# A transformer pair in one program: the convolution's norm moves one block earlier among a delta rule's blocks, and the first two slabs of the second output projection swap halves

## The reference, cut to what matters

```python
def conformer_conv(a, gate, dw_w, dw_b, ln_g, ln_b):
    y = a * jax.nn.sigmoid(gate)
    y = causal_depthwise_conv(y, dw_w) + dw_b
    y = layer_norm(y, ln_g, ln_b)
    return jax.nn.silu(y)
...
    def step(state, inp):
        u_n, w_n, qk_n, qd_n, kd_n, cd_n = inp
        u = u_n - jnp.einsum("bhck,bhkv->bhcv", w_n, state)
        o = jnp.einsum("bhck,bhkv->bhcv", qd_n, state) + jnp.einsum("bhij,bhjv->bhiv", qk_n, u)
        state = cd_n[..., None, None] * state + jnp.einsum("bhck,bhcv->bhkv", kd_n, u)
        return state, o
...
    o = rms_norm(o, norm_g) * jax.nn.silu(g)
...
        mix = jnp.concatenate([y_a, y_b, y_c], axis=-1)
        x = x + jnp.einsum("bte,ed->btd", mix, w_out[l])
```

## Time and profile before

| what | us |
|---|---|
| median of 3 runs | 3643.97 |
| lowest, highest | 3641.48, 3645.7 |
| the profiled execution, its time | 3644.55 |
| the profiled execution, its span | 3642.7 |
| PE matmul busy | 3535.9 (97%) |
| DVE busy | 1470.6 (40%) |
| POOL busy | 1136.8 (31%) |
| ACT busy | 963.0 (26%) |

### The profile page before, as it was taken

How to read it: one execution, slowest core, us unless ns; L and a number is a source line. 1 busy time by engine, 2 the same in 40 slices (tenths; PEclk the granted TensorE clock), 3 DMA queues, 4 the chain that set the end, 5 groups by cost and what they waited for, 6 DMA issues and landing times.

```text
span 3642.7 us, 52855 instructions
## 1 busy us (share of the span) xinstructions
PE 3535.9 (97%) x20076; PEld 2935.7 (81%) x20076; DVE 1470.6 (40%) x2553; ACT 963.0 (26%) x1684; POOL 1136.8 (31%) x1499
## 2 busy tenths in 40 slices
PE   8999889999999999999999999999999999999998
PEld 6777767888888878899999878797777788888886
DVE  7865455211112163312121473837876521111214
ACT  5243533211111142111111333115663311111112
POOL 4432044322222253222222442310025532222223
PEclk9999999999999999999999999999999999999999
DMA  3111122111111121111111232111024221111113
GB/s 123 41 43 57 34 87 76 59 51 45 53 42 51 40 82 51 48 46 41 52 41 52 58 134 77 41 30 39 30 91 150 87 63 48 51 42 52 46 44 100
DMA packets 79620, 218.51 MB, mean 60 GB/s; under 512 B 18912, under 2 KB 19040, under 8 KB 78816
## 3 DMA queue, kind: packets, MB, share of 16 engines
q1 hardware_dynamic: 61792, 173.35, 15.8%
q10 hardware_dynamic: 17664, 42.88, 3.2%
HBM read 195.67 MB, written 19.46 MB: 59 GB/s over the span
## 4 chain that ended last, share of the span: by engine, by line
issue 61%; POOL 24%; PE 8%; DVE 5%; ACT 1%; POOLq 1%; DMA 0%; ACTq 0%; SPq 0%; DVEq 0%
POOL w_lo L568 24%; PE acc L726 2%; DVE cv_acc L1725 2%; PE acc L727 2%; PE acc L728 2%; PE acc L1267 0%; PE acc L1262 0%; POOLq L572 0%; DVE cvo L1807 0%; DVE ssq L676 0%; DMA x<-in_x_dram 0%; PE acc L1356 0%; PE acc L1277 0%; PE acc L1400 0%; DVE tmp L688 0%
## 5 line engine op out<-in xcount | busy, mean ns | idle before, releaser
L568 POOL TENSOR_TENSOR w_lo<-w_raw,w_hi 128x256 fp32r<-128x256 f32 (+3 forms) x1480 | 1116.1, 786 | 2389.3 <-ACT w_hi L538 2388.9
L726 PE MATMUL acc<-h_hi,w_hi 128*128 128x512 f32 (+1 forms) x3520 | 1304.8, 371 | 25.2 <-POOL w_lo L568 17.6
L727 PE MATMUL acc<-h_lo,w_hi 128*128 128x512 f32 (+1 forms) x3520 | 1303.4, 370 | 0.0
L728 PE MATMUL acc<-h_hi,w_lo 128*128 128x512 f32 (+1 forms) x3520 | 1298.0, 369 | 0.0
L726 PEld LDWEIGHTS acc<-h_hi,w_hi 128*128 128x128 f32 x3520 | 665.2, 189 | 152.8 <-issue 22.1
L727 PEld LDWEIGHTS acc<-h_lo,w_hi 128*128 128x128 f32 x3520 | 664.7, 189 | 118.3 <-issue 1.9
L728 PEld LDWEIGHTS acc<-h_hi,w_lo 128*128 128x128 f32 x3520 | 665.6, 189 | 115.4
L538 ACT CAST w_hi<-w_raw 128x1024 fp32r<-128x1024 f32 (+3 forms) x370 | 346.3, 936 | 1225.0 <-PE acc L728 1205.3
L998 DVE TENSOR_TENSOR ff_hi<-tmp,acc 128x512 f32 (+3 forms) x154 | 94.5, 614 | 1101.6 <-PE acc L728 1066.1
L726 PE MATMUL acc<-ff_hi,w_hi 128*128 128x512 f32 (+1 forms) x1232 | 449.5, 365 | 5.5 <-POOL w_lo L568 2.9
L728 PE MATMUL acc<-ff_hi,w_lo 128*128 128x512 f32 (+1 forms) x1232 | 447.0, 363 | 0.0
(11 more groups left out here) (377 smaller groups left out, 3017.7 us busy)
## 6 DMA issues: line engine op xcount, KB each, us to landing
w_raw<-in_ffn_w_dram SPq DMA_DIRECT2D x94, 512.0 KB, 3.5
w_raw<-in_w_in_dram SPq DMA_DIRECT2D x60, 512.0 KB, 3.6
w_raw<-in_w_out_dram SPq DMA_DIRECT2D x32, 512.0 KB, 3.5
w_raw<-in_ffn_w_dram SPq DMA_DIRECT2D x48, 320.0 KB, 2.9
w_raw<-in_w_gate_dram SPq DMA_DIRECT2D x24, 512.0 KB, 3.5
w_raw<-in_w_up_dram SPq DMA_DIRECT2D x24, 512.0 KB, 3.5
w_raw<-in_ffn_w_dram SPq DMA_DIRECT2D x32, 384.0 KB, 3.1
gates_kept<-gstage ACTq DMA_DIRECT2D x32, 256.0 KB, 2.0
```

The costliest lines, as they stand in the source:

```text
L568: pool.tensor_tensor(w_lo[:, j, a:a + step], w_raw[:, j, a:a + step], w_hi[:, j, a:a + step].bitcast(F32), ALU.subtract).then_inc(split_do ...
L726: pe.matmul(bank, wh, rh, start=(k == 0), stop=False)
L727: pe.matmul(bank, wh, rl, start=False, stop=False)
L728: ins = pe.matmul(bank, wl, rh, start=False, stop=(k == seg.kt - 1))
```

## The change

Four places in the first block, and one in the second.

- `SHARED` and `EXTRA`: m0 is computed before the levels that precede block 0, m1 at the end of block 0 (before: block 1), v0 at the end of block 1 (3), v1 ahead of s0 at the end of block 2 (4). Block 3 keeps only its spread, block 4 its spread and s1.
- DVE: `centred(0)` ahead of block 0 (before: in block 1), `centred(1)` in block 0 (2), `normed(0)` in block 2 (4), `normed(1)` in block 4 (5).
- ACT: both squares of `cv_acc` in block 1, behind the squares of o (before: one each in blocks 2 and 3); the roots v0 in block 1 and v1 in block 2 ahead of s0's; Silu and the high parts in block 5 (6).
- `pe_slab` takes a range of tiles `ks`, and `pe_last`, where `late` is given, runs tiles 0 to 3 of slab 0, tiles 0 to 3 of slab 1, then tiles 4 to 7 of slab 0 and of slab 1.

Nothing is added or left out in PE's, DVE's and POOL's instructions; ACT loads one table less.

```diff
--- before.py
+++ after.py
@@ -702,9 +702,10 @@
             split(0)
             dve.wait_ge(sem("consts_full"), 16)
 
-        def pe_slab(pe, seg, i, j, rhs, only=None, late=None, at=0):
+        def pe_slab(pe, seg, i, j, rhs, only=None, late=None, at=0, ks=None):
 
             n = len(seg.chunks)
+            ks = ks or range(seg.kt)
             fine = only is None
             if not fine:
                 pe.wait_ge(split_done, i * (2 * LOW_PIECES) + LOW_PIECES * (seg.n0 + j + 1))
@@ -716,7 +717,7 @@
                 elif seg.need[i, j, c]:
                     pe.wait_ge(acc_free[j], seg.need[i, j, c])
                 bank = acc[:, seg.bank(i, j, c), 0:w]
-                for k in range(seg.kt):
+                for k in ks:
                     if late:
                         late(c, k)
                     if fine and c == 0 and (k == 0 or seg.low_pieces(k) > seg.low_pieces(k - 1)):
@@ -726,7 +727,8 @@
                     pe.matmul(bank, wh, rh, start=(k == 0), stop=False)
                     pe.matmul(bank, wh, rl, start=False, stop=False)
                     ins = pe.matmul(bank, wl, rh, start=False, stop=(k == seg.kt - 1))
-                ins.then_inc(acc_full[j], 1)
+                if ks[-1] == seg.kt - 1:
+                    ins.then_inc(acc_full[j], 1)
 
         def pe_pairs(pe, seg, rhs, first=0):
 
@@ -766,10 +768,16 @@
                 else:
                     if then:
                         pe.wait_ge(sem("ff_" + then), len(FQ) * (len(segs[0].chunks) + 1))
-                    pe_slab(pe, seg, 0, 0, rhs, late=None if half else late)
+                    if late and not half:
+                        for ks in (range(seg.kt // 2), range(seg.kt // 2, seg.kt)):
+                            for j in range(2):
+                                pe_slab(pe, seg, 0, j, rhs, late=late, ks=ks)
+                    else:
+                        pe_slab(pe, seg, 0, 0, rhs)
                 if half:
                     pe_mean(pe, name, 0)
-                pe_slab(pe, seg, 0, 1, rhs)
+                if half or not late:
+                    pe_slab(pe, seg, 0, 1, rhs)
                 for i in range(1, seg.pairs):
                     for j in range(2):
                         pe_slab(pe, seg, i, j, rhs)
@@ -1168,7 +1176,7 @@
 
             return slice(2 * HEADS * (lv // 4), 2 * HEADS * (lv // 4) + 2 * HEADS)
 
-        SHARED = ("m0", "m1", "s0", "v0", "s1", "v1", "s2", "s3")
+        SHARED = ("m0", "m1", "v0", "v1", "s0", "s1", "s2", "s3")
 
         def pe_mix1(pe):
             h = (h_hi, h_lo)
@@ -1364,12 +1372,13 @@
                 ins = pe.matmul(acc[:, b, :], ones, odiag[n // 4][:, :, blk(n % 2)], start=True, stop=True)
                 ins.then_inc(sem("spread_full"), 1)
 
-            EXTRA = {0: ("m0",), 1: ("m1",), 2: ("s0",), 3: ("v0", 0), 4: (1, "s1", "v1"), 5: (2,), 6: (3, "s2")}
+            EXTRA = {0: ("m1",), 1: ("v0",), 2: ("v1", "s0"), 3: (0,), 4: (1, "s1"), 5: (2,), 6: (3, "s2")}
 
             pe.wait_ge(sem("x_solved"), 1)
             pe.wait_ge(sem("silu_done"), 12)
             prelude(0)
             turn_keys(0)
+            shared("m0")
             for lv in range(4):
                 level(lv)
             for b in range(2):
@@ -1635,7 +1644,7 @@
                 else:
                     act.activation(drs[:, cc(v)], acc[:, 4, :], ACT.Sqrt, bias=const("eps")).then_inc(sem("shared_taken"), 1)
 
-            ROOTS = {2: ("s0",), 3: ("v0",), 4: ("s1", "v1"), 6: ("s2",)}
+            ROOTS = {1: ("v0",), 2: ("v1", "s0"), 4: ("s1",), 6: ("s2",)}
             prelude(0)
             decayed_keys(0)
             for lv in range(4):
@@ -1657,14 +1666,15 @@
                     mix_high(1)
                 if n in (1, 3, 5, 7):
                     squares(n // 2)
-                if n in (2, 3):
-                    act.wait_ge(sem("cv_centred"), n - 1)
+                if n == 1:
                     act.wait_ge(sem("mix_hi"), 2)
                     act.wait_ge(sem("o_lo"), 2)
-                    act.activation(cv_sq[:, :, cc(n - 2)], cv_acc[:, :, cc(n - 2)], ACT.Square).then_inc(sem("cv_var_in"), 1)
+                    for c in range(2):
+                        act.wait_ge(sem("cv_centred"), c + 1)
+                        act.activation(cv_sq[:, :, cc(c)], cv_acc[:, :, cc(c)], ACT.Square).then_inc(sem("cv_var_in"), 1)
                 for name in ROOTS.get(n, ()):
                     root(name)
-                if n == 6:
+                if n == 5:
                     act.wait_ge(sem("cv_normed"), 1)
                     for ct in range(2):
                         own.mark(act.activation(cv_acc[:, ct, :], cv_acc[:, ct, :], ACT.Silu,
@@ -1930,6 +1940,7 @@
             prelude_decay(0)
             prelude_products(0)
             prelude_queries(0)
+            centred(0)
             for n in range(NBLK):
                 cur = n % 2
                 dve.wait_ge(sem("ks_full"), n + 1)
@@ -1958,17 +1969,18 @@
                 own.wait()
                 dve.sem_inc(sem("state_full"), 1)
                 prelude_queries(n + 1)
-                if n in (1, 2):
-                    centred(n - 1)
+                if n == 0:
+                    centred(1)
+                if n == 2:
+                    normed(0)
                 if n == 3:
                     diagonals(0)
                 if n == 4:
                     scaled(0, 1)
-                    normed(0)
+                    normed(1)
                 if n == 5:
                     scaled(1, 1)
                     diagonals(1)
-                    normed(1)
                 if n == 6:
                     scaled(2, 1)
```

## The result

The changed kernel takes **3650.0 us** (median of 20 runs, 3645.6 to 3652.2) against 3643.3 of the kernel before in the same session (20 runs): ratio 1.0018, 95% interval 1.0011 to 1.0025. It is 6.8 slower, outside the range of 3640.0 to 3647.0. The profiled execution took 3651.75. All times are in us. Of the executions further down, one of the kernel before took 3900.1 at a mean granted clock of 0.84, and is left out of every ratio.

A forecast was written before the change was run, and what follows sets the result against it. TensorE, 97% busy, was taken as the bound; 2.15 + 2.35 - 1.05 - 2.1 - 1.45 - 2.8 + 0.6 + 1.7 = -0.6 took the profiled 3644.55 to 3643.95, median 3643.4; range 3640.0 to 3647.0.

The forecast's parts named there:

- H, the clock: New idle at ends of blocks 1 and 2 and before the fifth tile: one new slow-clock stretch, +1.7.
- A: Block 1, v0 instead of m1: v0 waits for ACT's square and TensorE idles 2.6, +2.15.
- B: Block 2, v1 then s0: s0 waits for ACT's root of v1, behind a table load, +2.35.
- C: Block 3, v0 gone: 1.82 saved, 0.75 waited for the spread's diagonal, -1.05.
- D: Block 4, v1 gone: its full-clock length and its wait saved, 1.82 + 0.27, -2.1.
- E: Blocks 5 and 6: normed(1) moved saves 2.1, but Silu delays block 7's exponential, leaving -1.45.
- F: Gate of the first output projection: POOL's low parts ready earlier, fifth tile starts 2.8 sooner, -2.8.
- G: Second block's output projection: split hides nothing, second slab waits about 1.0, residual later, +0.6.
- first rival: Block 1 and before the fifth tile: clock stays down in two long stretches, +7.9, 3651.9; chance 0.03.
- out2a's new wait: Sign of being right: a new wait of 1 us in the second slab of the second block's output projection.
- The fifth tile: Gate of the first output projection: starting 1 to 4 us sooner was a sign of being right.
- Rival 3: Block 6: POOL's pair and DVE hold each other up, two DVE instructions give +2.2, 3645.6; chance 0.12.

The follow-up runs named there:

- change + filler: Changed kernel plus three unread TensorE products, two ahead of v0 in block 1, one ahead of s0 in block 2: 3645.6, ratio 1.0002 to the kernel before.
- order runs: The two runs "order" and "order 2", without the split, first square ahead of the copy of o: 3642.2 and 3637.5.
- before + wait + filler: Kernel before, with TensorE waiting ahead of m1 for an extra unread ScalarE square and two unread products inside that wait: 3645.8, ratio 1.0005.
- the Silu run: "order 2" with Silu and the two high parts back in block 6 on ScalarE: 3640.5, ratio 0.9986 to the kernel before.
- order 2: "order" with v1 moved from the end of block 2 to block 3, ahead of the spread: 3637.5, ratio 0.9981 to the kernel before.
- order: Changed kernel without the split, first square ahead of the copy of o, s0 ahead of v1 in block 2: 3642.2, ratio 0.9993 to the kernel before.
- the two runs above: "change + filler", and the kernel before with TensorE waiting ahead of m1 for an extra unread square: ratios 1.0002 and 1.0010.
- square first: Changed kernel with ScalarE making v0's square ahead of its copy of o in block 1: 3642.4, ratio 0.9993 to the kernel before.
- the pair in the kernel before: Kernel before with an extra unread square awaited ahead of m1, without and with two unread products in the wait: 3648.0 and 3645.8.

## Why the prediction was wrong

The step that failed is **H, the clock**, a term of the sum that was mis-sized: taken as +1.7, bounds -1.7 to +3.4. The parts of the delta rule without it (A to F) came to -2.9; measured was +5.5. The difference, **8.4**, is left for the clock, five times the term and far outside its bounds. The rest of the sum was close wherever a run shows the block at full clock:

- **A**, +2.15: the wait is 2.66 (2.6 forecast), and where the clock holds block 1 is 2.18 longer. In the changed kernel it is 3.63 longer.
- **B**, +2.35: with the clock held, 2.35. In the changed kernel 3.15. The table load takes 1.28 and the root begins at once, so the row was the right one to go by. The Trainium skill (ScalarE: Activation LUTs, What ACT_TABLE_LOAD costs), with a drain on top, would have asked for 3.7; the one clean block shows 2.35.
- **C**, -1.05: block 3 got 1.53 longer, since it runs at 1.2 GHz from 426 to 433. v0 is gone from it and the wait for the diagonal is there, 0.71 (forecast 0.75). But no run shows this block clean with this order, so the size of C stays an estimate. In "change + filler", with a shorter stretch there, it is 0.7 longer.
- **D**, -2.1: -2.87 against a block that had a fall in it. Clean against clean it is 12.23 (order runs) against 14.46 (before + wait + filler): -2.2.
- **E**, -1.45: TensorE's wait of 2.08 for DVE is gone, as said, and where the clock holds Silu does push the exponential, by 0.63 (the Silu run; the prediction's 2.1 less 1.45 makes 0.65). In the changed kernel itself it does not, since the slow blocks give ScalarE time. Blocks 5 and 6 in "order 2" are 26.15 against 27.38, -1.2 with a slow start of the last stretch in it; in the changed kernel they are +1.7, because the falls of 454 and 471 stand in them.
- **F**, -2.8: the wait for POOL's convolution low parts is gone; the last part is 1.62 shorter, though most of it ran at 1.2 GHz, from 485 to 494. Where the clock was lower for less of it ("order") it is 3.2 shorter.
- **G**, +0.6: 0 to 0.3. The wait in the second slab is there (0.2 to 0.8, forecast 1.0), but the third slab's shrinks from 1.0 to about 0.6.

Why H was so small: it was sized by one row, a short stretch, and one new fall was counted. The changed kernel has five where the kernel before has three, and three of them are long. The prediction named the right mechanism as its first rival and gave it 0.03, with the argument that the work behind each new idle is dense. That the rival's 3651.9 lies within 2 of the median is in part luck: it had two long stretches, behind the idle times of block 1 and of the gate, and the long ones stand at 426, at 454 and ahead of the gate, at 484. The work is dense at 426 to 433 and at 454 to 460, 7.00 of 7.00 and 6.00 of 6.00 busy. Half a clock makes any work look denser, but the same matmuls in the kernel before are as dense at full clock: in its second profile all fourteen half-microsecond slices from 416.5 to 423.5 are full, of which the first and the last are

```profile
416.50:417.00 0.50, 0.50 (x6) 0.50 (x6) 0.00 (x0) 0.47 (x2) 0.00 (x0) 1.00 0.00 0
423.00:423.50 0.50, 0.50 (x7) 0.50 (x6) 0.00 (x0) 0.50 (x2) 0.00 (x0) 1.00 0.00 0
```

So dense work behind a place did not keep the clock up there. The argument should have looked at what TensorE does just before. Of the changed kernel's five falls one comes inside the wait for the square (409), one behind the wait of 2.41 for the spread (470.5), and three inside a group of sixteen one-column matmuls or within 0.4 behind it (426, 453.5, 484). The kernel before has the same groups without a fall in them, so a group alone does not do it; what else must come together is not shown. That one wait changes falls elsewhere is shown by "square first" (3.9 gained in unedited blocks) and by the pair in the kernel before (a fall bought off in block 1 and back in block 3). What decides in which block they come stays open.

A check of the size: 31 - 10 = some 21 more at 1.2 GHz. At the 0.43 to 0.46 of the two runs above that is 9 to 9.5, against the 8.4. The Trainium skill (TensorE: Matmul & The Clock Gate, HAM oscillation) takes half of the throttled time as lost; an estimate by that is 10, and this trace, with 8.4, has somewhat less. That some of the slow time lay in front of waits that end with another engine would explain it, and is not shown.

Of the signs named beforehand, v0's wait, s0's wait, block 4, block 6's wait for DVE, the low parts and out2a's new wait came right. The fifth tile came 5.7 later and not 1 to 4 sooner, with stretches at half clock over 4 long: what the text had named as the sign of its being wrong. Rival 3 (POOL beside DVE) did not happen: of DVE's instructions in block 6, u's (0.68) and the decayed product (0.69) ran beside POOL's pair (473.78, 4.70) at their usual length, and the queries' product came behind it.

## What to carry to other kernels

In a chain of short matmuls on TensorE with waits between them, price a new wait of 2 to 3 us at 1.4 to 2.5 times its length (the two cases here: 2.57 cost 3.70 in its own block, and taking 2.66 away gave 6.7). Where the profile before has stretches at half clock, as here three, let the range have more and longer ones in it. Fix the wait by its cause (who queues what ahead of the producer), before moving work between blocks; a product that nobody reads, put into the wait, is the cheap test whether the clock is in it. Read the granted clock per stretch before a block's length is compared with another's, since a "saved" 2.9, as in block 4, can be 2.2 and a slow clock that moved on.

## What was not expected of the hardware

- The pattern of falls repeated to 0.05 in each block in two profiles of each of two kernels, though moving one instruction shifted most of it. It is no fixed property: leaving the split out, an edit far behind, exchanged a stretch of 3 and one of 7.
- Useless work can make a kernel faster: three products of 0.9 to 1.0 gave 2.95 by the trace and 3.5 to 4.4 by the medians.
- TensorE was at 1.2 GHz while 100% busy for 7 (426 to 433), with a wait of only 1.34 before it; the clock fell inside the sixteen one-column matmuls that followed the wait.
